# Output projection with its first column half finished by the fourth of six products

## What is computed

```python
def trunk_layer(x, mod, mixer, moe, ln1_g, ln1_b, ln2_g, ln2_b, alpha, ...):
    sh1, sc1, g1, sh2, sc2, g2 = jnp.split(mod[:, None, :].astype(x.dtype), 6, axis=-1)
    h = ln_plain(x) * (1 + sc1) + sh1
    mix, kd, vd, s_f, s_b = mixer(h, ...)          # ends with  merged @ w_out
    x = ln_affine(alpha * x + g1 * mix, ln1_g, ln1_b)
    h = ln_plain(x) * (1 + sc2) + sh2
    x = ln_affine(alpha * x + g2 * moe(h), ln2_g, ln2_b)

def ec_moe(h, w_router, w_gate, w_up, w_down):
    aff = jax.nn.softmax((xt @ w_router).astype(jnp.float32), axis=-1)
    cap = CAPACITY_FACTOR * n // N_EXPERTS
    gate, idx = lax.top_k(aff.T, cap)
    xe = jnp.take(xt, idx, axis=0)
    hid = silu(xe @ w_gate) * (xe @ w_up)          # 16 experts, 1024 -> 2816
    ye = (hid @ w_down) * gate                     # 2816 -> 1024
```

## Time and profile before

| | before |
|---|---|
| median of 3 runs | 1796.67 us (1795.52 to 1797.03) |
| span of the profiled execution | 1793.6 us |
| PE busy | 1654.7 us (92%) |
| DVE busy | 507.3 us (28%) |
| ACT busy | 300.0 us (17%) |
| HBM read | 634.17 MB, 356 GB/s over the span |
| first product of expert 0 | at 532.25 us |

### The profile page before, as it was taken

The page is one execution under the profiler, slowest core; times in us unless marked ns, Lnnn a source line. Parts: engine busy times, 40 slices in busy tenths (PEclk is TensorE's granted clock), DMA queues, the critical chain, the costliest instruction groups (busy, mean ns, idle before and its releaser), DMA issues.

```text
span 1793.6 us, 19164 instructions
## 1 busy us (share of the span) xinstructions
PE 1654.7 (92%) x7876; PEld 772.9 (43%) x7876; DVE 507.3 (28%) x971; ACT 300.0 (17%) x641; POOL 57.9 (3%) x89
## 2 busy tenths in 40 slices
PE   6999999999999999998888989898888989899897
PEld 3777777788863333332323223232223223233332
DVE  4575647765771111010101101010101101011113
ACT  2543354563331000000000000000000000000001
POOL 3110000021000000000000000000000000000001
PEclk9999999999999999999999999999999999999999
DMA  9962233137599999999999999999999999999996
GB/s 348 363 222 100 89 126 107 67 129 259 222 378 406 409 430 432 428 430 429 432 428 429 435 428 431 428 429 431 430 430 428 434 428 431 428 430 429 429 430 270
DMA packets 67966, 638.53 MB, mean 356 GB/s; under 512 B 6272, under 2 KB 6456, under 8 KB 37328
## 3 DMA queue, kind: packets, MB, share of 16 engines
q1 hardware_dynamic: 64240, 629.83, 84.3%
q0 software_dynamic: 3680, 8.06, 1.4%
HBM read 634.17 MB, written 3.70 MB: 356 GB/s over the span
## 4 chain that ended last, share of the span: by engine, by line
DMA 48%; PE 48%; SPq 1%; DVE 1%; ACT 1%; issue 0%; ACTq 0%
DMA ring<-in_w_exp_up 23%; DMA ring<-in_w_exp_gate 21%; PE banks L935 18%; PE banks L1344 16%; PE banks L1469 4%; DMA ring<-in_w_exp_down 4%; PE banks L933 1%; SPq L590 1%; PE banks L1326 1%; PE banks L886 1%; PE banks L1122 1%; PE banks L944 1%; DMA ring<-in_w_mod 1%; PE banks L1143 1%; PE banks L931 1%; PE banks L1079 1%
## 5 line engine op out<-in xcount | busy, mean ns | idle before, releaser
L1344 PE MATMUL banks<-ring,O 128*64 128x512 f32 (+1 forms) x2844 | 620.2, 584 | 57.1 <-DMA ring<-in_w_exp_gate 39.7
L1344 PEld LDWEIGHTS banks<-ring,O 128*64 128x64 f32 x2844 | 195.0, 136 | 487.0 <-issue 372.0
L1469 PE MATMUL banks<-ring,O 128*64 128x512 f32 x1400 | 309.9, 595 | 33.1 <-DMA ring<-in_w_exp_down 26.4
L2346 DVE TENSOR_TENSOR X<-X,banks 128x512 f32<-128x512 f32 x90 | 61.9, 687 | 582.6 <-PE banks L1326 582.6
L1469 PEld LDWEIGHTS banks<-ring,O 128*64 128x64 f32 x1400 | 97.7, 137 | 234.2 <-issue 182.1
L935 PE MATMUL banks<-slot_parts,X_parts 128*128 128x512 f32 x672 | 191.0, 405 | 0.0
L1794 ACT ACTIVATE O<-banks 128x512 f32<-128x512 f32 (+1 forms) x48 | 23.7, 562 | 694.0 <-PE banks L1344 694.0
L935 PEld LDWEIGHTS banks<-slot_parts,X_parts 128*128 128x128 f32 x672 | 119.9, 188 | 31.8 <-issue 10.7
L1924 DVE TENSOR_TENSOR slot_parts<-ring,slot_parts 128x512 fp32r<-128x512 f32 x168 | 106.2, 695 | 14.4 <-ACT slot_parts L1525 14.0
L2368 DVE TENSOR_TENSOR O<-banks,O 128x512 f32<-128x512 f32 x32 | 20.7, 686 | 307.0 <-PE banks L1469 307.0
L935 PE MATMUL banks<-slot_parts,H_parts 128*128 128x512 f32 x384 | 107.0, 391 | 0.0
(11 more groups left out here) (332 smaller groups left out, 1171.6 us busy)
## 6 DMA issues: line engine op xcount, KB each, us to landing
ring<-in_w_exp_up SPq DMA_DIRECT2D x60, 2816.0 KB, 33.8
ring<-in_w_exp_gate SPq DMA_DIRECT2D x43, 2816.0 KB, 34.5
ring<-in_w_exp_down SPq DMA_DIRECT2D x28, 3072.0 KB, 28.9
ring<-in_w_exp_down SPq DMA_DIRECT2D x13, 4096.0 KB, 31.7
ring<-in_w_in SPq DMA_DIRECT2D x16, 2048.0 KB, 8.3
ring<-in_w_exp_down SPq DMA_DIRECT2D x25, 1024.0 KB, 31.4
ring<-in_w_exp_gate SPq DMA_DIRECT2D x15, 1408.0 KB, 31.7
N<-in_w_exp_gate SPq DMA_DIRECT2D x15, 1408.0 KB, 37.4
```

Source lines behind the costliest of these rows:

```text
L1344: x = pe.matmul(banks[64 * w:64 * w + 64, 3 * m + b, 0:(i1 - i0) * P], xeT[:, 2 * (k % 4) + k // 4, :], w4[:, w, i0 * P:i1 * P], start=(k ...
L1469: x = pe.matmul(banks[64 * w:64 * w + 64, (4 if last else 6) + dc, :], hidT[:, i, 64 * w:64 * w + 64], rows[:, w, dc * BANK:(dc + 1) * BAN ...
L2346: dve.tensor_tensor(dst, dst, banks[:, 3 + n % 3 if spread or last else 6 + n % 2, :], ALU.add).then_inc(acc_done, 1)
```

## The change

The order of the six products goes from (0,0) (0,1) (1,0) (1,1) (2,0) (2,1) to (0,0) (0,1) (1,0) (2,0) (1,1) (2,1). The fourth product is now the context tile's first half, and the fifth the second latent tile's second half. What depends on it follows: SP waits for the last product of column half 0 (now the fourth, before the fifth), PE waits for the context tile's turned columns before the fourth product, POOL waits for the copy of the fifth, and DVE makes the norms of the second latent tile after the fifth copy, with the sixth between.

```diff
-WO_ORDER = [(n, h) for n in range(T) for h in range(2)]
+WO_ORDER = [(0, 0), (0, 1), (1, 0), (2, 0), (1, 1), (2, 1)]
...
-            sp.wait_ge(job_done, J_WO[-2] + 1)
+            sp.wait_ge(job_done, last_job_of(WO_FIRST) + 1)
...
-            wait_job_copied(pool, J_WO[3])
+            wait_job_copied(pool, J_WO[4])
...
             job(J_WO[2])
+            wait_tile(pe, F_M, 2)
             job(J_WO[3])
             spread_sums()
-            wait_tile(pe, F_M, 2)
             job(J_WO[4])
...
             job_copy(J_WO[3])
-            layer_norms(1, J_WO[4])
+            job_copy(J_WO[4])
+            layer_norms(1, J_WO[5])
...
-            half_stats(0, 0)
-            job_copy(J_WO[5])
-            first_norm(2, (1,))
+            first_norm(2)
```

## The result

The changed kernel takes 1803.01 us (median of 8 runs, 1801.54 to 1803.51) against 1796.79 us for the kernel before (8 runs). The ratio is 1.0032, with a 95% interval of 1.0023 to 1.0041: between 4.1 and 7.4 us slower. The forecast was 1802.8 us.

A forecast was written before the change was run, and what follows sets the result against it. The prediction took a full-rate weight stream as the bound, its last pause set by expert 0's start; 4.55 us (late norm) plus 1.6 us (clock) gave 6.15 us on 1796.67, so 1802.8 us, 8 in 10 from 1798.5 to 1805.5.

The forecast's parts named there:

- What bounds the kernel: Whole kernel: weight stream at full rate from 588 us to 1740 us; its last pause hangs on when expert 0 begins.
- The two thin stretches: DMA at 536 to 543 and 580 to 588 us, 296 GB/s each: claimed to be waiting for PE to free space.
- The loads: SP's three expert 0 loads, issued 5.9 us sooner, near 498.5 us: gain costed at nothing, up to 4.1 us without PE's wait.
- The new pause ahead of expert 0's first release: Expected sign in DMA's windows: a new thin stretch ahead of 538 us.
- The norm: 4.55 us: Second latent tile: norm 5.96 us late, less 1.4 us to spare, so ACT's copy of turned columns starts 4.55 us later.
- The clock: 1.6 us: PE after an expected 5.3 us idle gap: granted clock falls to 0.50, costing 1.6 us; bounds nothing to 2.9 us.
- The rival without a fall: PE's clock does not fall, or is back within the gap: 4.55 us alone, 1801.2 us; chance 0.19.
- The sum: Start of expert 0 and the end both 6.15 us later (4.55 + 1.6): expert 0 at about 538.4 us, median 1802.8 us.
- 3.07 us between span and median: Kernel before: its median, 1796.67 us, taken to stand 3.07 us above the profiled span of 1793.6 us.
- Part given back by the stream: Thin stretches at 536 and 580 us due to small loads; only some 2 us lost, 1798.7 us; chance 0.12.
- Faster by the loads: Stream is the limit from 500 us on; filling its stretch takes 4.1 us off, 1792.6 us; chance 0.04.
- The clock low for longer: Routing up to 532 us on PE: two more low-clock stretches, 2 x 1.6 us more, 1806 us; chance 0.08.

## Why the prediction was right

**What bounds the kernel.** Right, and now shown: a full-rate stream whose last pause ends when PE gives back space in expert 0. The two thin stretches were waits for PE, since late loads fill them, and about 5 us fit into them (4.6 by 15 us at 296 instead of 428 GB/s). The later loads brought out what the prediction did not need: once the loads are more than about 5 us late, the stream sets the end, though expert 0 is on time.

**The loads.** Costed at nothing; the changed kernel with and without them differs by 0.6 us in the medians, inside the error, and by 0.08 us on PE. The new pause ahead of expert 0's first release is there (0 GB/s from 538 to 540), and a second that I had not named, at 528 to 530 us, ahead of the load that waits for the third tile's normalisation. That load starts 6.28 us later than before, with expert 0's delay; but it is as late in the changed kernel with late loads, and there DMA moves 401 GB/s from 528 to 530 us. So this pause needs both the late norm and the early loads, and it is here, between 520 and 536 us, that most of their gain is lost. The prediction had put that at the wait from 536 to 543 us: the value was right, the place was not.

**The norm: 4.55 us.** From the end of the sixth product to ACT's copy it took 0.64 us before and takes 5.16 after, which is 4.52; with the clock kept up, 4.49 us arrive at expert 0. The step that sized it, 5.96 us less the idle time that ACT had, held to 0.06 us.

**The clock: 1.6 us.** Right in kind, a little small: 1.89 us come off when the gap is filled. PE's gap is 4.84 us and not 5.3: the row of 0.45 us from which I took the turning of tile 0 holds four of its eight matmuls, and all eight take 1.04 us. I had taken the cost of one fall under back-to-back matmuls. Here PE turns tile 1, does the products without use (L1226) and the router's products at half speed: 1.94, 1.49 and 1.62 us instead of 1.06, 0.83 and 1.07. The granted clock reads 0.50 from 513.0 us on, before PE starts again, and comes back between 519.5 and 520, so PE works for over 4 us at half clock; at 815.85 us it fell behind PE's restart and read 0.50 from about 817 to 820, so PE spent less of its work there. That this difference makes the 0.3 us is plausible and not tested. The rival without a fall had its 1801.2 us; the kernel in which the fall was taken out measured 1800.7.

**The sum.** Expert 0 starts 6.38 us later by the traces, counted from the sixth product, and the medians stand 6.22 apart, against 6.15 forecast. The two profiled spans differ by 7.9 us. That is no second effect that repeats in the medians: the profiled execution of the changed kernel took 1803.28 us with a span of 1801.5, so 1.8 us lie around the span. If the same lay around the span of before (an estimate), that execution took 1795.4 us and was as quick as the quickest of the runs, 1795.52. My 3.07 us between span and median held 1.3 us of such luck. Since I added the sum to the median, it did no harm. Where in the stream that 1.6 us of difference between the two executions (1261.4 against 1263.0 us from expert 0 to the end) lies is open; kernels that start on time spread as widely, from 1261.4 to 1263.1.

**The rivals.** Part given back by the stream (1798.7 us): no; the loss of 4.1 to 7.4 us excludes its 2 us, and the stretch at 536 us was a wait, as late loads fill it. The rival was priced with 4.55 us alone; with the 1.6 us of the clock in it, its hole would have been 3.6 us and its time 1800.2. Faster by the loads (1792.6 us): no, excluded by the late loads that cost nothing. The clock low for longer (1806 us): no; it is 1.00 again in the window from 520 us, after one stretch of low clock.

## What to carry to other kernels

A stream at full rate to the end does not mean that an earlier load helps: look for thin stretches between the load and the point where the stream stops pausing. They are room that swallows a delay (here about 5 us), and an earlier load gains nothing either, as long as the next release comes no sooner: DMA then runs dry ahead of it. When products are put in another order, ask of each what its consumer had to spare: the second latent norm had 1.4 us, was made 6 us later, and the difference went straight to the end. And a wait of some microseconds that opens on PE can cost more than the delay that it stands for, when the granted clock falls with it; if it can't be avoided, try products without use in it, which gave 1.9 us back here.

## What was not expected of the hardware

The fall of the clock does not go by the length of the one wait that the profile names. In the kernel before it fell behind a wait of 2.11 us, with waits of 1.89 and 0.22 us in the 19 us ahead of it; in the changed kernel with 8 products in the gap it stayed at 1.00 through 3.05 us of idle time, and with 4 it fell behind 3.94 us. The last two are one run each, and what decides is open. And a single fall cost 1.6 us of chain where matmuls stood back to back, but 1.9 us in the changed kernel and 1.4 us (28.52 - 27.09) in the one with 4 products. In the last the clock fell between 515.5 and 516 us, behind PE's restart at 515.48, and came back between 519 and 519.5; in the changed kernel it was down before the restart.
